# Decay factors and products of the gated-linear-attention heads, one place later in two engines' rows

## The reference, cut to what matters

```python
proj = h @ w_in
q, k, v, a_lr, r = jnp.split(proj, ...)
log_a = jax.nn.log_sigmoid((a_lr @ w_gate + b_gate).astype(jnp.float32)) / GLA_GATE_TAU
...
g = jnp.cumsum(chunks(log_a, GLA_DK), axis=3)
...
a_intra = jnp.einsum('bhnid,bhnjd->bhnij', qc * jnp.exp(g - g_mid), kc * jnp.exp(g_mid - g))
...
q_inter = jnp.moveaxis(qc * jnp.exp(g), 2, 0)
k_state = jnp.moveaxis(kc * jnp.exp(g_last - g), 2, 0)
decay = jnp.moveaxis(jnp.exp(g_last[:, :, :, 0]), 2, 0)
```

## Time and profile before

| what | value |
|---|---|
| median of 3 runs | 1456.23 us (1451.13 to 1456.42) |
| profiled execution: its time | 1454.96 us |
| its span, first to last instruction | 1453.2 us |
| mean granted TensorE clock | 0.987 of full |
| busy: PE / DVE / ACT / POOL | 96% / 36% / 36% / 33% |
| share of the DMA engines, last third of the span | 99% in most slices |

### The profile page before, as it was taken

One profiled execution on the slowest core, in us unless ns is written; L12 is line 12 of the kernel. 1 busy time (PEld: TensorE's weight loads), 2 busy tenths in 40 slices (PEclk: granted clock), 3 DMA queues, 4 the chain that ended last, 5 costly groups with the idle time before them and its releaser, 6 DMA issues. The chain is left out here.

```text
span 1453.2 us, 26659 instructions
## 1 busy us (share of the span) xinstructions
PE 1391.0 (96%) x11116; PEld 1045.8 (72%) x11116; DVE 525.9 (36%) x1256; ACT 521.8 (36%) x1096; POOL 474.9 (33%) x457
## 2 busy tenths in 40 slices
PE   7999999999999999999999999999999999989986
PEld 6788886667888888888778786876666665656553
DVE  3102117742221200221334604264554554454345
ACT  4325438853322222222445533333223222222222
POOL 5334546543544444444455854410000000000000
PEclk9999999999999999999989999999999999999998
DMA  5133225313133034132132221669999999999994
GB/s 187 60 117 116 96 79 161 104 47 128 58 116 116 30 116 144 59 116 85 64 116 73 100 74 58 240 253 375 414 419 420 419 419 420 419 419 420 420 419 175
DMA packets 89561, 293.22 MB, mean 202 GB/s; under 512 B 9308, under 2 KB 38144, under 8 KB 64864
## 3 DMA queue, kind: packets, MB, share of 16 engines
q1 hardware_dynamic: 89040, 290.35, 51.8%
q0 software_dynamic: 288, 1.05, 0.2%
q10 hardware_dynamic: 112, 0.09, 0.0%
HBM read 289.27 MB, written 2.13 MB: 201 GB/s over the span
## 5 line engine op out<-in xcount | busy, mean ns | idle before, releaser
L496 POOL TENSOR_TENSOR wring_halves<-wring,wring_halves 128x512 fp32r<-128x512 f32 x274 | 356.7, 1307 | 378.2 <-ACT wring_halves L491 376.5
L491 ACT CAST wring_halves<-wring 128x512 fp32r<-128x512 f32 x274 | 168.0, 620 | 433.8 <-PE ps L1219 410.8
L1217 PE MATMUL ps<-wring_halves,big_halves 128*128 128x512 f32 x612 | 241.4, 394 | 4.5 <-POOL wring_halves L496 3.7
L1217 PE MATMUL ps<-hT_halves,wring_halves 128*128 128x512 f32 x480 | 188.2, 392 | 1.7 <-DVE big_halves L1975 0.9
L1218 PE MATMUL ps<-big_halves,wring_halves 128*128 128x512 f32 x480 | 187.4, 390 | 0.0
L1219 PE MATMUL ps<-hT_halves,wring_halves 128*128 128x512 f32 x480 | 187.2, 390 | 0.0
L2663 POOL TENSOR_TENSOR rstd<-rstd,half 128x1 f32<-128x1 f32 (+1 forms) x21 | 13.6, 647 | 508.6 <-DVE rstd L2616 479.6
L1218 PE MATMUL ps<-wring_halves,hT_halves 128*128 128x512 f32 x436 | 170.4, 391 | 0.0
L1219 PE MATMUL ps<-wring_halves,hT_halves 128*128 128x512 f32 x436 | 170.3, 391 | 0.0
L1217 PEld LDWEIGHTS ps<-wring_halves,big_halves 128*128 128x128 f32 x612 | 115.3, 188 | 33.2 <-POOL wring_halves L496 7.2
L1736 PE MATMUL ps<-xn,fixed 128*128 128x512 f32 x256 | 120.0, 612 | 0.4 <-DVE fixed L2411 0.4
(11 more groups left out here) (348 smaller groups left out, 1995.6 us busy)
## 6 DMA issues: line engine op xcount, KB each, us to landing
big<-in_moe_w_dram SPq DMA_DIRECT2D x90, 1024.0 KB, 25.2
wring<-in_moe_w_dram SPq DMA_DIRECT2D x70, 1024.0 KB, 25.7
wring<-in_ffn_w_in_dram SPq DMA_DIRECT2D x22, 1024.0 KB, 7.2
hT<-in_moe_w_dram SPq DMA_DIRECT2D x20, 1024.0 KB, 25.0
wring<-in_fox_w_in_dram SPq DMA_DIRECT2D x7, 2048.0 KB, 8.7
wring<-in_gla_w_in_dram SPq DMA_DIRECT2D x6, 2048.0 KB, 8.0
mkv<-in_moe_w_dram SPq DMA_DIRECT2D x12, 1024.0 KB, 25.8
wring<-in_ffn_w_out_dram SPq DMA_DIRECT2D x4, 2048.0 KB, 7.8
```

The costliest lines, as they stand in the source:

```text
L491: act.copy(hi, src).then_inc(s_hi, 1)
L496: pool.tensor_tensor(lo, src, hi, ALU.subtract).then_inc(s_lo, 1)
L1217: pe.matmul(out, lhs[1], rhs[0], start=start, stop=False)
```

## The change

It adds one to each entry of two lists.

```diff
         F_LOG = [15, 20, 25, 30]
-        F_EXP = [17, 22, 27, 32]
-        F_POOL = [20, 25, 30, 35]
+        F_EXP = [18, 23, 28, 33]
+        F_POOL = [21, 26, 31, 36]
         HEAD_AT = [(0, 1), (0, 4), (0, 6), (1, 1)]
```

## The result

The changed kernel takes 1457.92 us (median of 16 runs, 1452.36 to 1460.91), the kernel before 1454.32 us in as many (1448.10 to 1458.07). The ratio is 1.0026 with a 95% interval of 1.0015 to 1.0037: 3.8 us slower, between 2.2 and 5.4. The forecast was a move of 3.2 us. Its absolute figure, 1459.4, was added to the median of three runs shown beforehand, 1456.23; beside the 16 runs taken with the changed kernel the same move gives 1457.5.

The account below looks back on a forecast made before the run. PE, busy 96%, bounds the kernel, but the loop over ACT, DVE and POOL paces this stage. Chunk 31 3.2 us later on 1454.96 gives 1458.2, plus 1.27 for the runs' median: 1459.4 us, range 1454.5 to 1463.5.

Parts of the forecast that it names:

- The bound and its size: PE in this stage: only its waits for POOL's low halves can move, about 3.6 us, 0.25%, at most to win.
- Low half 20 and head 0's products: POOL: low half 20 takes 1.96 us, products start at 793.8 and take 4.6; chunk 21 comes 2.5 us late.
- The loop: ACT, DVE and POOL from one head's factors to the next: 15.65 us instead of 14.49, with POOL's side the longer.
- The rule: POOL beside DVE's running sum: whoever comes second blocks; low half 20 would lose up to 2.20 us. Not used in the forecast.
- The sum: PE's chunk 31 and all behind it come 3.2 us later, between +0.5 and +5.8 us, through to the end.
- A: PE's stalls in the stage vanish and nothing takes their place: 3.6 us less, 1452.6 us; chance 4%.
- C: Nothing to be seen: POOL is less disturbed, the short ends hold, 1456.7 us; chance 14%.
- B: PE's clock falls to 0.50 behind stalls: 1461.0 us if behind chunk 31 alone (35%), 1464.2 in full (7%).
- "No cost" for the high half ahead of the factors: ACT: high half 22 done by about 792.5 while ACT waits for DVE, costing nothing and removing PE's wait at chunk 22.

Follow-up runs that it names:

- The best run: Kernel before, lists unchanged, with DVE's step L2231 moved ahead of `decayed_q`: stretch 49.71 us, ratio 0.9986, and 0.9977 the second time.
- The transfer and memset runs: Changed kernel with L2749's transfer behind the last head's products: ratio 1.0014; with one or three memsets before products of heads 1 to 3: stretch 56.12, 57.38 us.
- the run with L2231 early: Kernel before with DVE's step L2231 moved ahead of `decayed_q`, lists as before: ratio 0.9986, repeated 0.9977; stretch 49.71 us both times.

## Why the prediction was right

**The bound and its size.** It said that PE moves only where it waits for a low half, and that 3.6 us was all to be won. The best run won 2.8 us of stretch.

**Low half 20 and head 0's products.** Predicted to start at 793.8, 0.8 us behind the end of low half 20; they started at 793.90 in a trace that was 0.79 us late before chunk 17, so at 793.1 like for like. The low half took 1.29 us, not the 1.96 taken: it started 0.17 ahead of the running sum, not inside it. The prediction's own rows had it that way round (low half from 791.1, sum from 792.23). What brought the sum 1.0 us forward is the DVE step ahead of it, L2233: 0.69 us here, 1.67 before, beside POOL's products. The three products took 4.76 us against 4.6. Chunk 21 came at 799.2 like for like, against 799.8.

**The loop.** Predicted 15.65 us, on POOL's side; measured 16.14, on POOL's side. Up to the high half behind the logarithm nothing changed, as said (4.77 and 2.48). The terms that were mis-sized partly cancel. The low half took 1.25 instead of 1.65, and the products of head 1 took 5.55 (809.24 to 814.79) instead of 4.7, outside the upper bound of 5.12. These are head 1's products in the kernel before, from which the 5.12 was read, and DVE's running sum beside them:

```profile
803.77 1.29 POOL L2752 TENSOR_TENSOR big<-big,arena 128x512 f32<-128x512 f32 x1
805.14 1.62 POOL L2754 TENSOR_TENSOR big<-big,arena 128x512 f32<-128x512 f32 x1
806.72 2.20 POOL L2755 TENSOR_TENSOR big<-big,arena 128x512 f32<-128x512 f32 x1
```

```profile
805.65 2.19 DVE L2234 TENSOR_TENSOR_SCAN big<-xn,big 128x512 f32<-128x512 f32 x1
```

One product started inside the sum before, too: the last, 2.20 us long, which ended 1.1 behind the sum. In the changed kernel it is the first (2.21), and the two behind it lie beside DVE's two differences (1.61 and 1.71, against 1.29 and 1.62). That makes the 0.43 by which 5.12 was passed.

**The rule.** The prediction weighed the rule of the Trainium skill (SBUF — State Buffer, "Who interferes with whom"), that a DVE instruction with two SBUF inputs and a GpSimd instruction that reads SBUF exclude each other, and went by the rows instead, read as a loss of 1.3 us spread over two low halves. But those rows show the block as well: the two low halves end at 791.60 + 3.91 = 795.51, 1.1 us behind the sum's end at 794.43, which is where a product started inside the sum ends in the runs. The row of low half 25 with only ACT's list moved fits this too. The transfer and memset runs show the rule at work in this case: a product started inside the running sum ends 1.1 us behind it, whenever it starts, and a memset, which reads nothing, runs beside it. But of “whoever comes second blocks”, as the prediction put it, only POOL's side came out for the sum: the sum never waited, though low half 20 was under way when it began (2.19 us as always), while L2233, another DVE step with two inputs, did wait for POOL (1.67 us against 0.69). The rule was also named for the wrong instruction: low half 20 lost nothing, the product behind the low half did, 0.9 us at heads 1 and 2. That the loop came out only 0.5 too short is in part luck: the products were taken 0.85 too short, the low half 0.4 too long.

**The sum.** 3.2 us predicted for chunk 31 and all behind it; the stretch shows 3.57, and the times 3.8 (2.2 to 5.4). The two rounds of the loop were together 1.0 us longer than predicted, and chunk 21 came 0.6 earlier; that these nearly cancel is luck, not foresight.

**The rivals.** A (the stalls vanish) did not come; the run with L2231 early shows what it would have needed. C (nothing to be seen) neither. B had two parts. That the clock can fall behind stalls of this length came true: in each of the two traces of the changed kernel it fell once, and it stayed up behind the other long wait (1.76 us in the first, 2.21 in the second). That a fall behind one of the first two stalls is eaten up by the next wait is seen as well: 56.11 and 56.08 us with the fall at different stalls. No trace has a fall behind the third, to which the prediction gave 35%, so its price for the stretch was not seen. In the second trace the third wait was at its full length, and the clock did not fall.

**The parts.** "No cost" for the high half ahead of the factors was right. That it takes away PE's wait at chunk 22 was right too, but in the run with that edit alone the time came back as a longer wait at chunk 25.

## What to carry to other kernels

Before moving work to an earlier place in one engine's row, ask what its input is queued behind on the engine that makes it: here 1.3 us of POOL's work brought an idle time of 4.55 us with it, because a cast stood behind a logarithm. When several engines hand one head on to the next, measure the loop (start of a step to its next start) and set it against the bounding engine's time per round. Only what lies on the loop's longest side counts: one DVE step taken off it gained 2.8 us of the stretch, the best order of the three lists alone 1.3. Where a gain is near the spread of whole executions, measure a fixed stretch of the trace: it repeated to 0.03 us here.

## What the runs showed of the hardware

- A POOL `tensor_tensor` that starts during DVE's running sum (2.20 us, two inputs from SBUF) ends 1.1 us behind the sum's end, wherever in the sum it started, whereas one begun 0.17 us ahead of the sum took its usual 1.29 us. The sum itself takes 2.19 to 2.21 us in either case. So 0.8 us of POOL work taken away, or 0.6 us added, in front of it changed nothing.
- The blocked time lies inside an instruction's duration, not in the idle time ahead of it, so it reads like a slower instruction. DVE's two differences (L2236, L2238) took 1.60 and 1.77 us in the changed kernel, where a POOL product was under way when they came, and 0.69 and 0.68 us in the run with three memsets, where they came before the product; there the product was the longer one, 1.85 us.
- PE's clock fell to 0.50 behind a stall of 1.76 us in one trace and of 2.20 in another, though dense matmuls of 512 columns surrounded both. The length of the stall alone does not decide it: one of 2.21 us in the second trace of the changed kernel, one of 1.90 us with only ACT's list moved, and six of 0.66 to 1.77 us with only POOL's list moved brought no fall within the stretch. What does decide it is not shown here.
